# Norms by token tile, low halves kept in the weight ring, router weights loaded first, in a two-layer encoder kernel

## The reference, cut to what matters

```python
for l in range(DEPTH):                       # DEPTH = 2
    hn = rms_norm(h, attn_norm[l])
    p = hn @ w_in[l]                         # 1024 x (mixer columns and 3 x 1024 gate columns)
    ...                                      # retention, RWKV-7 and latent attention, three gated branches
    h = h + merged @ w_o[l]
    hn = rms_norm(h, ffn_norm[l])
    if l % 2 == 0:
        f = swiglu(hn, ffn_w_gate, ffn_w_up, ffn_w_down)      # 1024 -> 2816 -> 1024
    else:
        f = moe_swiglu(hn, moe_router, moe_w_gate, moe_w_up, moe_w_down)  # top 2 of 8 experts, 3584 wide
    h = h + f
return rms_norm(h, final_norm)
```

## Time and profile before

| what | value |
|---|---|
| device time, median of 3 runs | 2127.91 us (2127.08 to 2136.88) |
| the profiled execution's own time | 2126.94 us |
| its span | 2125.1 us |
| PE busy | 2000.5 us (94%) |
| DVE busy | 1377.9 us (65%) |
| ACT busy | 1111.0 us (52%) |
| granted TensorE clock, mean | 0.973 |
| HBM traffic | 480.06 MB read |
| chain that ended last | PE 85%, DVE 6%, ACT 4%, issue 2% |

### The profile page before, as it was taken

One profiled execution on the slowest core, in us unless ns is written; L12 is line 12 of the kernel. 1 busy time (PEld: TensorE's weight loads), 2 busy tenths in 40 slices (PEclk: granted clock), 3 DMA queues, 4 the chain that ended last, 5 costly groups with the idle time before them and its releaser, 6 DMA issues.

```text
span 2125.1 us, 23988 instructions
## 1 busy us (share of the span) xinstructions
PE 2000.5 (94%) x9114; PEld 1532.6 (72%) x9114; DVE 1377.9 (65%) x1377; ACT 1111.0 (52%) x1089; POOL 103.9 (5%) x124
## 2 busy tenths in 40 slices
PE   6999999989989989999789999999999999999997
PEld 5856666468877756665468788887878878788786
DVE  4672444335445753344169888888888888888886
ACT  4465111144334554111157677777767777776774
POOL 1340000000000520000000000000000000000000
PEclk9999998999999999998989999999999999999999
DMA  9533021444446432032089898998989989899993
GB/s 328 169 119 110 10 119 40 166 171 165 179 161 203 139 119 79 1 119 80 11 293 365 324 345 333 346 364 317 365 325 352 358 325 369 325 347 351 329 375 145
DMA packets 181490, 485.66 MB, mean 229 GB/s; under 512 B 5880, under 2 KB 12660, under 8 KB 172600
## 3 DMA queue, kind: packets, MB, share of 16 engines
q1 hardware_dynamic: 176256, 475.53, 61.1%
q0 software_dynamic: 1488, 5.57, 0.8%
q10 hardware_dynamic: 3688, 3.74, 0.7%
HBM read 480.06 MB, written 1.05 MB: 226 GB/s over the span
## 4 chain that ended last, share of the span: by engine, by line
PE 85%; DVE 6%; ACT 4%; issue 2%; POOL 1%; DMA 1%; ACTq 0%; DVEq 0%; SPq 0%
PE bank L1431 40%; PE bank L1011 17%; PE bank L1003 7%; PE bank L1111 6%; PE bank L1401 1%; PE bank L1385 1%; PE bank L1462 1%; DVE w_lo L1492 1%; PE bank L1215 1%; ACT w_hi L939 1%; PE bank L1295 1%; DMA ring<-moe_w_gate_dram 1%; DVE xg_lo L1919 1%; PE bank L1228 1%; DVE xterm L1492 1%
## 5 line engine op out<-in xcount | busy, mean ns | idle before, releaser
L1492 DVE TENSOR_TENSOR w_lo<-ring,w_hi 128x2048 fp32r<-128x2048 f32 x336 | 764.1, 2290 | 153.1 <-ACT w_hi L939 153.1
L939 ACT ACTIVATE w_hi<-ring 128x2048 fp32r<-128x2048 f32 x336 | 643.6, 1916 | 159.2 <-PE bank L1431 158.0
L1431 PE MATMUL bank<-w_hi,xg_hi 128*128 128x512 f32 x896 | 354.2, 395 | 9.2 <-DVE w_lo L1492 9.2
L1431 PE MATMUL bank<-w_hi,xg_lo 128*128 128x512 f32 x896 | 350.5, 391 | 0.0
L1431 PE MATMUL bank<-w_lo,xg_hi 128*128 128x512 f32 x896 | 350.4, 391 | 0.0
L1431 PEld LDWEIGHTS bank<-w_hi,xg_hi 128*128 128x128 f32 x896 | 169.5, 189 | 44.5 <-DVE w_lo L1492 10.4
L1431 PEld LDWEIGHTS bank<-w_hi,xg_lo 128*128 128x128 f32 x896 | 168.7, 188 | 35.6
L1431 PEld LDWEIGHTS bank<-w_lo,xg_hi 128*128 128x128 f32 x896 | 168.9, 189 | 34.1
L1431 PE MATMUL bank<-w_hi,ehT_hi 128*128 128x512 f32 x448 | 176.9, 395 | 3.6 <-DVE w_lo L1492 3.6
L1111 PE MATMUL bank<-ring,hnT 128*128 128x512 f32 x384 | 175.9, 599 | 0.0
L1431 PE MATMUL bank<-w_lo,ehT_hi 128*128 128x512 f32 x448 | 174.6, 390 | 0.0
(11 more groups left out here) (385 smaller groups left out, 2745.1 us busy)
## 6 DMA issues: line engine op xcount, KB each, us to landing
ring<-moe_w_gate_dram SPq DMA_DIRECT2D x56, 2048.0 KB, 7.8
ring<-moe_w_up_dram SPq DMA_DIRECT2D x56, 2048.0 KB, 8.4
ring<-moe_w_down_dram SPq DMA_DIRECT2D x56, 2048.0 KB, 7.9
ring<-w_in_dram SPq DMA_DIRECT2D x26, 2048.0 KB, 8.5
ring<-w_branch_dram SPq DMA_DIRECT2D x6, 2048.0 KB, 11.5
ring<-ffn_w_gate_dram SPq DMA_DIRECT2D x5, 2048.0 KB, 8.1
ring<-ffn_w_up_dram SPq DMA_DIRECT2D x5, 2048.0 KB, 8.1
ring<-ffn_w_down_dram SPq DMA_DIRECT2D x5, 2048.0 KB, 7.6
```

What stands on the lines that cost most here:

```text
L939: A.activation(w_hi[:, q % PARTS, :], ring[:, i, o:o + HALF], ACT.Copy).then_inc(s.hi_ready, 1)
L1431: ins = M(dst, a, w, start=start and n == 0, stop=stop and n == 2, skip_group_check=True)
L1492: return V.tensor_tensor(out_, a, b, op)
```

## The change

- Each norm runs tile by tile: square, root and scaling of tile 0, then of tile 1 (`norm_sums(m, t)`, `normalise(m, t, dst)`). TensorE transposes four blocks of one tile at a time (`transpose_rows`), and VectorE instead of ScalarE copies the bank out with the gains (`transposed`).
- The products with `w_o` come in the order o00, o10, o01, then the transposes of tile 0, then o11. The transposes of tile 1 stand inside the FFN's first gate block, or inside the router product (`second_rows`).
- The low halves are written over the weights in the ring (`ring_lo` is the same memory as `ring`, read as fp32r). The memory that this frees holds four rounded halves instead of two. A slot is now free when TensorE has used the panel.
- The last hidden block's transposes (`turn(5)`) move behind the first down panel; the `fd` products go tile by tile.
- Router weights get memory of their own and are loaded by POOL at the beginning instead of behind `o11.1`.
- The signal for the experts' first three panels moves from behind the routing to ahead of the additions of `o00`.
- Two one-element square roots are added on ScalarE, behind the dense FFN's last silu and behind the loop over experts.

```diff
-    out += [(f"o{u}{t}", V) for u in range(2) for t in range(T)]
-    out += [(f"fT{q}", A if l else V) for q in range(4)]
+    out += [(n, V) for n in ("o00", "o10", "o01", "fT00", "fT01", "o11", "fT10", "fT11")]
...
-    i_hi = sb("i_hi", [P, 2, HALF], F32R, where=B + 16384)
-    i_lo = sb("i_lo", [P, 2, HALF], F32R, where=B + 32768)
+    i_hi = sb("i_hi", [P, 4, HALF], F32R, where=B + 16384)
...
-    f_hi = sb("f_hi", [P, 2, HALF], F32R, where=pr_at)
-    f_lo = sb("f_lo", [P, 2, HALF], F32R, where=pr_at + 16384)
+    fxT = sb("fxT", [P, KD, SEQ], where=B + 45056)
+    f_hi = sb("f_hi", [P, 4, HALF], F32R, where=pr_at)
...
-        if kind.startswith("ffn"):
-            return s.f_lo_ready, 2 * (n - FIRST_FFN + 1)
-        if kind == "in":
-            return s.i_lo_ready, 2 * (9 * l + j + 1)
-        job = {"lora": f"g1.{l}", "mla": f"mk11.{l}", "gate": f"gt{2 * j + 1}.{l}",
+        if kind == "ffn_down" and j < 5:
+            return s.f_half_used, 12 + 2 * (j + 1)
+        job = {"in": f"in{j}_1.{l}", "ffn_gate": f"fg{j}1.0", "ffn_up": f"fu{j}1.0", "ffn_down": "fd11.0",
+               "lora": f"g1.{l}", "mla": f"mk11.{l}", "gate": f"gt{2 * j + 1}.{l}",
                "branch": f"br{j}11.{l}", "o": f"o{j}1.{l}"}[kind]
         return s.product_ready, JOB_AT[job] + 1
...
+        pool.dma_start(router[:], moe_router[0].rearrange("(c p) n -> p c n", p=P)).then_inc(s.router_loaded, 16)
...
+        def norm_sums(m, t):
+
+            own.step(A.activation(hn[:, t, :], h[:, t, :], ACT.Square, accum_out=stat[:, 0, t:t + 1]), s.sumsq_ready)
+            act.wait_ge(s.var_ready, T * m + t + 1)
+            own.step(A.activation(stat[:, 0, t:t + 1], stat[:, 0, t:t + 1], ACT.Sqrt), s.root_ready)
...
-                if q > 1:
-                    in_half_used(act, l, q - 2)
-                own.step(A.activation(i_hi[:, q % 2, 0:width], src, ACT.Copy), s.i_hi_ready)
+                if q > 3:
+                    in_half_used(act, l, q - 4)
...
+                        if j == 5:
+                            own.step(A.activation(den[:, 0, 0:1], C("ident", 0, 1), ACT.Sqrt))
...
+        A.activation(den[:, 0, 0:1], C("ident", 0, 1), ACT.Sqrt)
...
-            pe.wait_ge(s.hn_ready, 2 * T * l + T)
-            transpose_in("nT{}." + str(l), hn)
+            for u in range(2):
+                for t in range(T):
+                    pe.wait_ge(s.hn_ready, 2 * T * l + t + 1)
+                    transpose_rows(f"nT{t}{u}.{l}", hn, t, u)
...
+            o_slots = [panel("o") for u in range(2)]
+            project(f"o00.{l}", gT, o_slots[0], KD, 512, 0)
+            project(f"o10.{l}", gT, o_slots[1], KD, 512, 0)
+            project(f"o01.{l}", gT, o_slots[0], KD, 512, 1)
+            pe.wait_ge(s.hn_ready, 2 * T * l + T + 1)
             for u in range(2):
-                slot = panel("o")
-                for t in range(T):
-                    project(f"o{u}{t}.{l}", gT, slot, KD, 512, t)
-            pe.wait_ge(s.hn_ready, 2 * T * l + 2 * T)
-            transpose_in("fT{}." + str(l), hn, blocks=l == 1)
-            read_out(pe, f"fT3.{l}")
+                transpose_rows(f"fT0{u}.{l}", hn, 0, u, blocks=l == 1)
+            project(f"o11.{l}", gT, o_slots[1], KD, 512, 1)
+
+            def second_rows():
+                pe.wait_ge(s.hn_ready, 2 * T * l + 2 * T)
+                for u in range(2):
+                    transpose_rows(f"fT1{u}.{l}", hn, 1, u, blocks=l == 1)
+
             if l == 0:
...
+                        order = [(r, t) for r in range(2) for t in range(T)]
+                        if j == g == 0:
+                            order = [(r, t) for t in range(T) for r in range(2)]
+                        for r, t in order:
+                            q = 4 * j + 2 * g + r
+                            if j == g == 0:
+                                if r == t == 0:
+                                    pe.wait_ge(s.f_x_lo_ready, 2)
+                                if r == 1 and t == 0:
+                                    second_rows()
+                                if t == 1:
+                                    pe.wait_ge(s.f_x_lo_ready, 3 + r)
+                            ffn_split(q)
...
+                        turn(j - 1)
+                outs = [(u, t, bank(f"fd{u}{t}.0")) for t in range(T) for u in range(2)]
                 for j in range(6):
+                    used[0] += 1
+                    if j == 1:
+                        turn(5)
                     read_out(pe, f"hT{j}1.0")
...
+            if t:
+                second_rows()
+            read_out(pe, f"fT{t}1.1")
...
+        def normalise(m, t, dst):
+
+            cell = stat[:, 0, t:t + 1]
+            dve.wait_ge(s.sumsq_ready, T * m + t + 1)
+            step(V.tensor_scalar(cell, cell, 1.0 / D, EPS, ALU.mult, ALU.add), s.var_ready)
+            dve.wait_ge(s.root_ready, T * m + t + 1)
+            step(V.reciprocal(cell, cell))
+            settle()
+            step(V.tensor_scalar(dst[:, t, :], h[:, t, :], cell, None, ALU.mult), s.hn_ready)
+
+        def transposed(name, l, g, t, u, dst):
+
+            b = product(dve, f"{name}{t}{u}.{l}")
+            free(tt(dst[:, 4 * u:4 * u + 4, t * P:(t + 1) * P], b[:].rearrange("p (c n) -> p c n", c=4),
+                    wide(gains[:, l, g, 4 * u:4 * u + 4], P), ALU.mult), f"{name}{t}{u}.{l}")
...
+                transposed("nT", l, 0, 0, u, hnT)
+                in_lo(u)
+                ix_low(0, u)
+                transposed("nT", l, 0, 1, u, hnT)
+                ix_low(1, u)
...
+            if l == DEPTH - 1:
+                V.tensor_copy(smax[:, 1, :], smax[:, 0, :]).then_inc(s.lo_ready, 2 * RING)
...
-            normalise(2 * l + 1, hn)
+                add_to_h(f"o{u}0.{l}", 0, u)
+            normalise(2 * l + 1, 0, hn)
+            add_to_h(f"o01.{l}", 1, 0)
+            for u in range(2):
+                transposed("fT", l, 1, 0, u, fx)
+            for u in range(2 if l == 0 else 0):
+                fx_low(0, u)
+            add_to_h(f"o11.{l}", 1, 1)
+            normalise(2 * l + 1, 1, hn)
+            for u in range(2):
+                transposed("fT", l, 1, 1, u, fx)
+                if l == 0:
+                    fx_low(1, u)
```

223 lines of the change are left out of this document (101 added, 122 removed).

## The result

| | before | changed |
|---|---|---|
| median, 20 runs each | 2139.75 us (2127.08 to 2146.42) | 2122.36 us (2107.17 to 2136.64) |
| ratio | | 0.9921, 95% interval 0.9898 to 0.9945 |
| profiled execution, span | 2126.94, 2125.1 | 2115.81, 2114.0 |

The change makes the kernel 17 us faster, 12 to 22 by the interval. I had forecast 2104, from 24.3 us of gain off 2127.9. One further run of before, beside experiments 3 and 8, took 2935 us at a clock of 0.646 and is left out of their ratios. Two things are to be explained: the median of before's 20 runs lies 12 us above that of the three I had, and the gain is smaller than the sum.

The account below looks back on a forecast made before the run. TensorE, busy for 94% of the span, was taken as the bound, so only its waits could be won. Terms 7.9 + 1.3 + 0.8 + 2.5 + 2.2 + 8.4 + 1.2 = 24.3 us off 2127.9 gave 2104, range 2098 to 2115.

Parts of the forecast that it names:

- The base: Before's median, taken as 1.0 us above the profiled execution of 2126.94, so gains were counted off 2127.9.
- FFN norm: Norm before layer 0's dense FFN: tile order removes TensorE's waits; gain 7.9 us, bounds 5 and 8.7.
- Up to down: Dense FFN, up blocks to down projection: TensorE waits 2.6 us for fu5's product; gain 1.3, plus 0.8 for the clock.
- Norm ahead of layer 1: Norm before layer 1's mixer: early table, tile order and four rounded halves gain 2.5 us, bounds 0.5 and 4.
- Layer 0's first panels: Deeper buffer removes waits of 1.21 and 0.74, tile order adds 0.3; gain 2.2 us, from 0.5 to 3.
- Reading low halves from the ring should be free too: Split matmuls reading low halves from the ring cost nothing, since w_o products take 27.75 us with DMA busy or idle.
- Norm ahead of the experts: Layer 1, router to experts: 5.7 us from the router part and 2.7 from early panels; gain 8.4, bounds 5 and 9.5.
- End: Final norm: one table load of 1.28 us leaves the path; gain 1.2, between 0.5 and 1.5.
- A: VectorE becomes the path at the seams, so the gain is 14 us, time 2114; chance 0.22.
- B: The clock stays up where waits become shorter, 2.5 + 1.7 us more, time 2099; chance 0.10.
- C: The ring starves: panels released late land too late, 34 us lost with five, time 2138; chance 0.05.
- D: Expert panels stay late despite the moved signal, as SP waits for something else; 2.7 us lost, 2106; chance 0.04.

Follow-up runs that it names:

- experiments 3 and 8: 3: changed kernel, expert loop's last hidden-block transposes moved behind twelve down matmuls, 2093.9 us. 8: e8, e12 and e14, built on it.
- Experiments 1 and 2: 1: the changed kernel again beside before, unedited, 2120.07 against 2140.05 us. 2: before, unchanged, profiled a second time, 2141.4 us.
- Experiment 5: Changed kernel with w_o products, norm and all eight transposes back in the old order; 2129.8 us, ratio to before 0.9957.
- experiment 7: Two edits of the changed kernel: dense FFN's last transposes back ahead of the down projection, 2112.35 us; without the two early roots, 2110.27 us.
- e8: Changed kernel with expert-loop transposes moved, plus VectorE's product of fu5 ahead of the first down panel's low halves; 2091.2 us, ratio to before 0.9784.
- e12: e8 with low halves in buffers of their own and two rounded halves; 2090.47 us, ratio to before 0.9779.
- e14: e12 with GpSimd's MEMSET held back until both tiles of layer 1's first norm are scaled; 2098.53 us, ratio to before 0.9804.
- experiment 6: Two edits of the changed kernel: expert panels' signal back behind the routing, 2121.14 us; router weights' load back behind o11, 2129.93 us.

## Why the prediction was right or wrong

**The base (wrong, 12 us of the 18).** The step "the median of before is 1.0 above that execution" took three runs for the distribution. The 20 runs have their median 12.8 us above the profiled execution. Experiments 1 and 2 show where that lies: its expert loop had none of the falls of the clock, of which the second profile has six (8.9 us), and its mixer of layer 1 was 6.8 us shorter. From 2139.75 the measured stage gain of 18.6 to 19.2 gives 2121, and 2122 came. The rest of the miss, 5.1 to 5.7 us, is in the sum, in the terms below: in the first pair 1.0 in layer 0's first panels, 1.4 in the down projection, 2.2 in layer 1's panels and 1.2 at the router, less 0.7 that came better than forecast.

**FFN norm (right).** 7.9 forecast. TensorE's wait ahead of tile 1 was 0.59 where I had 0.6, nothing waited at the first FFN matmul, and from the first product to the start of the second pair of blocks 8.1 us were gone (84.15 to 76.08). Experiment 5 puts 6.8 of it, with the effect at the down projection, on the order.

**Up to down (size right, reason wrong).** 1.3 forecast, 1.2 measured (86.35 to 85.17 from the second pair to down), and a wait of 2.85 for the very product that I named. But experiment 7 shows that moving the transposes gave none of it. The 0.8 for the clock did not come: the down projection is 0.6 us longer than before's in the first profile, where the clock stays up, and 2.0 longer in the second, where it falls behind a wait of 2.76. Behind 1.84 it stayed up in e8 and fell in e12 and e14.

**Norm ahead of layer 1 (right in sum).** 2.5 forecast, 2.9 and 2.8 measured. Two of its parts were wrong. That for the table was empty, since the early load brought VectorE's scaling beside GpSimd's MEMSET. And the four rounded halves do not remove the wait of 1.28: it is 1.64, with two as with four. Both tiles are normed 1.9 us earlier relative to the down projection's end (forecast 2.1), and from there to the second panel are 12.5 us where I had 13.1 and before 13.4.

**Layer 0's first panels (too large).** 2.2 forecast, 1.2 measured. The step that failed is "the deeper buffer takes away the wait of 1.21": that wait grew to 1.55, and is 1.54 with two rounded halves; only the 0.73 went. The router's load delayed layer 0's first transposes by 0.5 (costed at 0, with 1 as the bound), and the low halves' reading took 1.1.

**"Reading low halves from the ring should be free too" (wrong, some 5 us).** I had argued from the `w_o` products. They did stay at 27.75 us, but they are whole fp32 products at another pace; the split matmuls grew from 389 to 400 ns. I had no row for that, and I gave it no bounds. My sign of being wrong, hi x lo matmuls longer than their neighbours, did come: 400 ns against 393 and 395.

**Norm ahead of the experts (mechanism right, 1.2 to 2.6 too large).** 8.4 forecast, 7.2 and 5.8 measured. The signal gave 2.6 of my 2.7. The router part came 0.9 later than forecast, with its second half at the lower clock, and the gather lost 0.7 more. That the router's early load was worth 10 us there, as the condition for the early signal, I had not seen.

**End (right).** 1.2 forecast, 1.5 measured, 1.0 of it by the early table.

**Rivals.** A came in part: TensorE waits for VectorE at the seams (2.85, 3.00 and 1.64 us), but the FFN's norm and layer 1's gave what I had forecast, and not A's 5 and 0.5; the first panels' 1.2 lie between A's 0.5 and my 2.2, and the router part's 7.2 and 5.8 between its 5 and my 8.4. B did, in a way that I had not priced: shorter waits left a higher mean clock (0.9705 against 0.966 on one chip, about 9 us of slow time), though the stages do not fall for it evenly. C did not come: TensorE never waited for a DMA inside the panels. D is refuted by experiment 6, where the wait comes back with the old signal.

On the table loads the sum went by 1.28 and not by the 2.66 of the Trainium skill (ScalarE: Activation LUTs, What ACT_TABLE_LOAD costs); experiment 7 measured 1.0 at the end, so this case speaks for the rows.

## What to carry to other kernels

Three runs and one profile are one draw of the clock: before a gain is counted off them, compare the mean granted clock of the profiled execution with that of the other runs, and look for short waits in a loop that repeats, since each is paid as a wait and, in some executions, once more as a fall of the clock behind it. Shortening waits around a long loop gave 17 us here in the medians (19 by the stages); one wait of 1.7 us inside the loop, eight times over, gave 26 in the medians (of two chips), of which 14.5 are the loop's own length without any fall. And a buffer that costs no space may cost pace: read the mean duration of a matmul group before and after, not only the waits.
